# Packed GLA level scores and softmax attention's values moved ahead of the transposes, in a two-layer decoder trunk

## What is computed

```
# GLA, per head and chunk: decayed scores, causal
A   = einsum('bihk,bjhk,bijhk->bhij', q, k, exp(b_i - b_j)) for j <= i
o   = (q * exp(b)) @ S + A @ v

# softmax attention, per block of 128 queries and a window of 256 keys
s = q @ k.T * HEAD_DIM ** -0.5 + bias ;  m = max(max(s), sink)
p = exp(s - m) ;  p = p / (sum(p) + exp(sink - m))
o = p @ v
```

## Time and profile before

| | us |
|---|---|
| median of 3 runs (2592.79 to 2594.49) | 2592.86 |
| the profiled execution, its own time | 2590.38 |
| span of its instructions | 2588.6 |
| its mean granted TensorE clock | 0.988 |
| PE, DVE, ACT busy | 2461.5, 1617.4, 1150.7 |
| GLA turns, about 56 to 565 us of the span | 509 |
| softmax attention, about 1384 to 1790 us of the span | 406 |

### The profile page before, as it was taken

One profiled execution on the slowest core, in us unless ns is written; L12 is line 12 of the kernel. 1 busy time (PEld: TensorE's weight loads), 2 busy tenths in 40 slices (PEclk: granted clock), 3 DMA queues, 4 the chain that ended last, 5 costly groups with the idle time before them and its releaser, 6 DMA issues. The chain is left out here.

```text
span 2588.6 us, 37710 instructions
## 1 busy us (share of the span) xinstructions
PE 2461.5 (95%) x15399; PEld 2149.4 (83%) x15399; DVE 1617.4 (62%) x2930; ACT 1150.7 (44%) x1822; POOL 44.1 (2%) x66
## 2 busy tenths in 40 slices
PE   7999999999999999999998999889999999999997
PEld 4777988877888889999996677767788889999996
DVE  5677567675765556766656665655766556655556
ACT  4655454544343334343336666654444333423333
POOL 0000000000000000000000000000000000000000
PEclk9999999999999999999999999989999999999998
DMA  4222222323433323322323232312332323332322
GB/s 158 66 66 89 83 93 98 126 93 97 157 103 120 107 86 97 127 84 89 115 83 95 97 114 71 95 50 79 115 126 95 103 94 98 98 118 79 98 82 97
DMA packets 83592, 255.18 MB, mean 99 GB/s; under 512 B 12963, under 2 KB 30540, under 8 KB 81484
## 3 DMA queue, kind: packets, MB, share of 16 engines
q1 hardware_dynamic: 64348, 202.45, 24.8%
q0 software_dynamic: 5792, 28.05, 3.4%
q10 hardware_dynamic: 13280, 22.28, 2.6%
HBM read 225.93 MB, written 26.74 MB: 98 GB/s over the span
## 5 line engine op out<-in xcount | busy, mean ns | idle before, releaser
L447 PE MATMUL banks<-act_hi,w_lo 128*128 128x272 f32 (+1 forms) x2952 | 972.7, 330 | 16.3 <-DVE act_lo L2295 6.7
L447 PE MATMUL banks<-act_hi,w_hi 128*128 128x272 f32 (+1 forms) x2952 | 958.6, 325 | 0.0
L447 PE MATMUL banks<-act_lo,w_hi 128*128 128x272 f32 (+1 forms) x2952 | 957.0, 324 | 0.0
L425 ACT ACTIVATE w_hi<-w_raw 128x1024 fp32r<-128x1024 f32 x366 | 380.8, 1055 | 691.6 <-PE banks L470 489.4
L430 DVE TENSOR_TENSOR w_lo<-w_raw,w_hi 128x1024 fp32r<-128x1024 f32 x366 | 443.1, 1223 | 367.0 <-ACT w_hi L425 366.7
L447 PEld LDWEIGHTS banks<-act_hi,w_lo 128*128 128x128 f32 x2952 | 557.5, 189 | 75.9 <-issue 20.9
L447 PEld LDWEIGHTS banks<-act_lo,w_hi 128*128 128x128 f32 x2952 | 558.6, 189 | 43.0 <-issue 1.7
L447 PEld LDWEIGHTS banks<-act_hi,w_hi 128*128 128x128 f32 x2952 | 557.1, 189 | 43.9
L482 DVE TENSOR_TENSOR acc<-acc,banks 128x272 f32<-128x272 f32 (+1 forms) x624 | 315.3, 519 | 191.2 <-PE banks L470 187.7
L470 PE MATMUL banks<-h_hi,w_lo 128*128 128x272 f32 (+1 forms) x1056 | 346.7, 328 | 23.0 <-DVE acc L482 13.5
L470 PE MATMUL banks<-h_hi,w_hi 128*128 128x272 f32 (+1 forms) x1056 | 344.6, 326 | 0.0
(11 more groups left out here) (243 smaller groups left out, 2601.6 us busy)
## 6 DMA issues: line engine op xcount, KB each, us to landing
w_raw<-wall SPq DMA_DIRECT2D x366, 512.0 KB, 3.6
normed<-h_scratch POOLq DMA_DIRECT2D x20, 352.0 KB, 4.2
h_scratch<-acc POOLq DMA_DIRECT2D x3, 2176.0 KB, 7.8
h_scratch<-acc POOLq DMA_DIRECT2D x3, 2048.0 KB, 7.7
gstates<-state ACTq DMA_DIRECT2D x4, 1024.0 KB, 6.5
gla_s<-gstates ACTq DMA_DIRECT2D x4, 1024.0 KB, 6.8
bias<-bias_scratch ACTq DMA_DIRECT2D x28, 128.0 KB, 2.4
bias_scratch<-bias_rows ACTq DMA_DIRECT2D x8, 383.0 KB
```

The lines of the kernel that those rows point to most:

```text
L425: nc.scalar.activation(WH[:, b % RING], WR[:, b % RAW], ACT.Copy).then_inc(w_hi, 1)
L447: last = nc.tensor.matmul(PS[:, bank, 0:n], w, a[X][:, k, o:o + n], start=(k == 0 and first), stop=(k == KT - 1 and w is wh and a is AH))
```

## The change

Four edits. In GLA, levels 1 to 4 stream only the right halves of the query blocks, 64 columns for each chunk in place of 128, into the first 256 columns of the bank, DVE's `masked` reads them there, and the zeroing of `QT[1]` goes. In `values` and in `s_values` the loop over e becomes the inner one, so that output partitions 0 to 63 and 64 to 127 take turns. PE's `s_new(d)` and `values(s - 3)` move from behind the projections of an iteration to between `scores(s)` and `transposed(s - 2)`. DVE's `s_new(d)` moves within w = 5 from behind `biased(s)` and the additions to ahead of `biased(s)`.

```diff
@@ -718,7 +718,12 @@
                         pe.wait_ge(dn_add, dn_end(("gla", u - 1)))
                     for c in range(HB):
                         x = slice(c * CH, (c + 1) * CH)
-                        last = nc.tensor.matmul(PS[:, 6 + s % 2, x], KTl[s % 2][:, x], QT[s % 2][:, x], start=True, stop=True)
+                        out, queries = PS[:, 6 + s % 2, x], QT[s % 2][:, x]
+                        if s:
+                            L = LEVELS[LV[s]]
+                            out = PS[:, 6 + s % 2, c * (CH // 2):(c + 1) * (CH // 2)].rearrange("p (n s) -> p n s", s=L)
+                            queries = queries.rearrange("p (n s) -> p n s", s=2 * L)[:, :, L:2 * L]
+                        last = nc.tensor.matmul(out, KTl[s % 2][:, x], queries, start=True, stop=True)
                     if s == 0 and X:
                         pe.wait_ge(v_ev_, VR[u, 1, 1])
                         x = slice(HP, HP + SAMP)
@@ -959,7 +964,7 @@
                 L = LEVELS[n]
                 nb = CH // (2 * L)
                 mask = MLEV[:, n].rearrange("p (n s) -> p n s", s=2 * L)[:, :, L:2 * L].unsqueeze(1).broadcast_to([P, HB, nb, L])
-                scores = PS[:, 6 + s % 2].rearrange("p (c n s) -> p c n s", c=HB, s=2 * L)[:, :, :, L:2 * L]
+                scores = PS[:, 6 + s % 2, 0:HP // 2].rearrange("p (c n s) -> p c n s", c=HB, s=L)
                 nc.vector.tensor_tensor(TM[:, s % 2].rearrange("p (c n s) -> p c n s", c=HB, s=L), scores, mask,
                                         ALU.mult).then_inc(lv_m, 1)
 
@@ -1002,7 +1007,6 @@
                         nc.vector.scalar_tensor_tensor(SB[:, b], SB[:, b], EL[:, 8 + b:9 + b], PS[:, 6 + b % 2, 0:DV],
                                                        ALU.mult, ALU.add).then_inc(ss_upd, 1)
 
-                nc.vector.memset(levels_of(QT[1], LEVELS[0])[0], 0.0)
                 nc.vector.memset(levels_of(KTl[1], LEVELS[0])[1], 0.0)
                 decayed(u, 1)
                 distance(u, 2)
@@ -1701,8 +1705,8 @@
                     if X and g % 8 == 2:
                         pe.wait_ge(xsa, 3 * (g // 8 - 4) + 1)
                 o, n = WIN * (g % 2), HD * (q % 8 // 4)
-                for e in range(2):
-                    for k in range(x0 // WIN, 2):
+                for k in range(x0 // WIN, 2):
+                    for e in range(2):
                         last = nc.tensor.matmul(PS[64 * e:64 * e + 64, 4, o:o + WIN], VTOK[:, blk - 1 + k, n:n + HD],
                                                 PT[:, g % 2, 2 * e + k], start=(k == x0 // WIN), stop=(k == 1))
                 last.then_inc(of, 1)
@@ -1789,10 +1793,12 @@
             def s_values(d):
                 pe.wait_ge(xte, 3 * d + 3)
                 pe.wait_ge(vc_in, 16 * (d // 2) + 16)
+                for b in range(NB):
+                    for e in range(2):
+                        y = slice(64 * e, 64 * e + 64)
+                        nc.tensor.matmul(PS[y, 7, 0:2 * SAMP], VCG[:, b], PX[:, b, y], start=(b == 0), stop=False)
                 for e in range(2):
                     y = slice(64 * e, 64 * e + 64)
-                    for b in range(NB):
-                        nc.tensor.matmul(PS[y, 7, 0:2 * SAMP], VCG[:, b], PX[:, b, y], start=(b == 0), stop=False)
                     last = nc.tensor.matmul(PS[y, 7, 0:2 * SAMP], VTOK[0:SAMP, 8, HD * (d // 2):HD * (d // 2) + HD], PXN[:, y],
                                             start=False, stop=True)
                 last.then_inc(xof, 1)
@@ -1807,6 +1813,10 @@
                     scores(s)
                 if s == 0:
                     pe.wait_ge(dn_add, dn_end((1, FG - 1)))
+                if d >= 0 and w == 4 and d < 4:
+                    s_new(d)
+                if 3 <= s < NIT + 3:
+                    values(s - 3)
                 if 2 <= s < NIT + 2:
                     transposed(s - 2)
                 if k == 0:
@@ -1823,10 +1833,6 @@
                 if w >= 4 and 1 <= k < 8:
                     units = len(down_units((k - 1) // 4)) // 4
                     downs(k - 1, range((w - 4) * units, (w - 3) * units))
-                if d >= 0 and w == 4 and d < 4:
-                    s_new(d)
-                if 3 <= s < NIT + 3:
-                    values(s - 3)
                 if s in (21, 22):
                     by_token(s - 21)
                 if d >= 0:
@@ -1944,6 +1950,8 @@
                     divided(s - 1)
                 if s >= 4 and s % 2 == 1:
                     lo(s - 4)
+                if d >= 0 and w == 5:
+                    s_new(d)
                 if s < NIT:
                     biased(s)
                 for q in range(1, PAIRS):
```

## The result

| | before | after |
|---|---|---|
| median, us (4 runs each, side by side) | 2592.82 (2590.65 to 2594.49) | 2637.07 (2635.33 to 2638.51) |
| span of the profiled execution | 2588.6 | 2635.2 |
| mean granted TensorE clock | 0.988 | 0.978 |

The ratio is 1.0175, with an interval from 1.0159 to 1.0190: slower by 44 us. The forecast was 2608, slower by 15, with a range that ended at 2622. The sign and the mechanism came out as forecast; the size is three times the forecast's and lies outside the range.

The account below looks back on a forecast made before the run. In-order PE, busy 2461.5 of 2588.6 us, was taken as the bound. New waits and clock, +23.6, less savings of 8.5, gave net +15.1 on 2592.9, so 2608 us; range 2588 to 2622.

Parts of the forecast that it names:

- Order in `values` 0, in `s_values` -5.2: Inner loop over e: nothing gained in `values`; each of four `s_values` calls 1.3 us shorter, -5.2 us in all.
- Shape changes -1.2: PE in attention: one change of stationary shape fewer where sample transposes follow the projection, -1.2 us.
- w = 7 with samples: Iterations 47, 55, 63 and 39: `values` wait 4.3 us for `lo` (6.5 at 39); together +9.8 us net.
- 21, 29, 31: Iterations at w = 5 and 7 with nothing late: `values` wait 0.5 us each for `lo`, +1.5 us.
- the clock: PE's granted clock at half after waits of 2 us or more: two added stretches of 3.4 us, +2 (0 to +7).
- the half X = 0: Iterations 5 to 25, norms and residual on DVE: eleven waits of 18.6 us in place of 13.0, +5.6 us.
- the iterations after w = 7 (41, 49, 57): DVE reaches its tail 2 us later because it waits for PE's down units: 0 to +5.4, middle taken, +2.7 us.
- s_new: -2.1: PE's four waits for DVE's `s_new`, 3.1 us, shrink to some 0.25 each when it moves ahead of `biased`: -2.1 us.
- 51, 59, 61: Iterations late by norm steps, most of it paid already by `te` or a bank: +2.0 us.
- A: Rival: waiting at `values` lets DVE catch up, so later waits vanish equally; only the 8.5 us gain remains, 2584; chance 0.15.
- C: Rival, half the waits: the half X = 0, 51, 59, 61 and the iterations after w = 7 cost nothing; 2596; chance 0.10.
- D: Rival, worse: all bounds at their upper end and no overlap in `s_values`, +28 us, 2621; chance 0.11.

Follow-up runs that it names:

- experiment 2: Kernel before, with only the loop order of e and k or b in `values` and `s_values` changed: 2585.47 us, ratio 0.9979.
- Experiment 7: Changed kernel plus 116 useless matmuls of 256 columns in 18 odd iterations, just ahead of the wait for `lo`: 2622.1 us, ratio 1.0114.
- Experiment 9: Changed kernel with DVE's norm steps of iterations 12 and 14 run ahead of its additions of the down units: 2633.88 us, ratio 1.0164.
- Experiment 5: Changed kernel with PE's `values` back at their old place, `s_new` still moved on both engines: 2585.55 us, ratio 0.9974.
- experiment 6: Changed kernel with `values` moved in even iterations only, at their old place in odd ones: 2583.87 us, ratio 0.9967.

## Why the forecast was right in kind and wrong in size

**Right.** *GLA at 0*: 0.9996. *Order in `values` 0, in `s_values` -5.2*: -5.4 alone; the call measured 1.34 us in the changed kernel, in three of the four, and 2.31 in the one that met a stretch at half clock. The Trainium skill's rule on row groups (TensorE: Matmul & The Clock Gate, The mechanism) would have kept 2.60; the measured 1.30 decides against it here. The forecast's step from `values` was weaker than it looks, though. Its 0.112 us is the pace of loads of 128 columns; `values` and `s_values` load 64, and in the earlier trace rows these go at (1619.54 - 1618.52) / 16 = 0.064. Eight at 0.064 take 0.5 us before the last one's way through, so the 0.67 of `values` shows no overlap by itself. That the price came out is in part luck; the overlap is shown by experiment 2. *Shape changes -1.2*: only in the aggregate, -6.6 us of work where -6.4 was forecast. *The mechanism*: odd iterations wait for `lo`, the change's own row of 62.7 us. *w = 7 with samples*: forecast 4.3, three times, and 6.5 at 39. Iteration 47 in the changed kernel, PE, then DVE and ACT:

```profile
1670.09 0.70 PE L1684 MATMUL banks<-kg,q 64*128 64x256 f32 x4
1675.21 0.96 PE L1710 MATMUL banks<-probs_t,v_tok 128*64 128x128 f32 x8 [4.42 <-DVE o_lo L1895]
```

```profile
1670.20 0.44 DVE L480 COPY acc<-banks 128x272 f32<-128x272 f32 x1 [0.32 <-PE banks L470]
...
1671.27 1.28 DVE L1923 CUSTOM_DVE_ANT_1 s_scores<-s_scores,s_mask,s_sinks 128x1024 f32<-128x1024 f32 x1
...
1672.89 1.17 ACT L2073 ACTIVATE s_scores<-s_scores,s_stats 128x1056 f32<-128x1056 f32 x1 [4.37 <-DVE s_stats L1927]
...
1674.25 0.36 ACT L2051 ACTIVATE o_hi<-banks 128x256 fp32r<-128x256 f32 x1
...
1674.64 0.42 DVE L1895 TENSOR_TENSOR o_lo<-banks,o_hi 128x256 fp32r<-128x256 f32 x1 [1.71 <-ACT o_hi L2051]
```

It is the chain of the earlier trace rows, instruction by instruction. The four waits measure 6.47, 4.42, 4.42 and 4.43. *21, 29, 31*: 1.9 us in all, forecast 1.5. *The banks' waits that go*: forecast -6, measured -8.9.

**Wrong 1, the clock: "I add two such stretches, at somewhat over half price: +2 (0 to +7)".** Measured +16. The step's premise was that most new waits stand where one was. But the waits grew in number (22 for `lo` where there were 3), and the stretches in number and length: nine of 37.5 us became sixteen of 88.7, ten of them 6.8 us long. The price was about right: 2 us for two stretches of 3.4 is 0.29 for each microsecond at half, where 0.32 to 0.36 came out. The count was wrong: 51 us more at half are fifteen stretches of 3.4, where the forecast had two. It was read from a single row of before, which has nine in the stage, two of them 6.8 us long. This is 14 of the 35 us that the forecast fell short in the stage.

**Wrong 2, the half X = 0: 18.6 us of new waits.** Measured 26.9 (4.12 at 5, 1.88 at 7, 0.87 at 8, 1.93 at 11, 3.42 at 13, 6.01 at 15, 1.99 at 17, 1.62 at 19, 3.09 at 23, 1.99 at 25), and none at 9, where 2.2 were forecast. With the 13.0 of before that is +13.9 in place of +5.6. The step that failed is "what counts is the chain from biased(s - 2) to the end of lo(s - 4) against PE's work": it took the chain's length from the kernel before. DVE in the kernel before, from biased(13) to lo at the head of 15:

```profile
1445.81 0.48 DVE L1875 CUSTOM_DVE_ANT_0 scores<-banks,bias,sinks_b 128x256 f32<-128x256 f32 x1
...
1450.29 0.69 DVE L480 COPY acc<-banks 128x512 f32<-128x512 f32 x1 [1.41 <-PE banks L470]
1451.68 0.69 DVE L480 COPY acc<-banks 128x512 f32<-128x512 f32 x1 [0.70 <-PE banks L470]
...
1457.74 0.41 DVE L1889 TENSOR_TENSOR o_lo<-banks,o_hi 128x256 fp32r<-128x256 f32 x1
```

The same in the changed kernel:

```profile
1451.30 0.47 DVE L1881 CUSTOM_DVE_ANT_0 scores<-banks,bias,sinks_b 128x256 f32<-128x256 f32 x1
...
1456.23 0.69 DVE L480 COPY acc<-banks 128x512 f32<-128x512 f32 x1 [4.04 <-PE banks L470]
1458.03 0.69 DVE L480 COPY acc<-banks 128x512 f32<-128x512 f32 x1 [1.11 <-PE banks L470]
...
1461.01 0.69 DVE L480 COPY acc<-banks 128x512 f32<-128x512 f32 x1 [1.43 <-PE banks L470]
1462.41 0.69 DVE L480 COPY acc<-banks 128x512 f32<-128x512 f32 x1 [0.70 <-PE banks L470]
1463.02 2.48 DVE L586 TENSOR_TENSOR act_lo<-normed,act_hi 128x1088 fp32r<-128x1088 f32 x2
1465.60 2.87 DVE L571 SCALAR_TENSOR_TENSOR normed<-acc,gain_cols,rstd 128x544 f32<-128x544 f32 x4
...
1468.47 0.40 DVE L1895 TENSOR_TENSOR o_lo<-banks,o_hi 128x256 fp32r<-128x256 f32 x1
```

The chain is 1468.87 - 1451.30 = 17.6 us, where it had been 1458.15 - 1445.81 = 12.3, and 7.3 of it are idle times in which DVE waits for PE, where there were 2.1: DVE's own work is 10.2 and 10.3. The largest of them, 4.04, stands where PE's down units go at half clock, 0.43 us apart in place of 0.23:

```profile
1454.28 0.63 PE L470 MATMUL banks<-o_hi,w_hi 128*128 128x512 f32 x1
1454.71 0.63 PE L470 MATMUL banks<-o_hi,w_lo 128*128 128x512 f32 x1
...
1459.89 0.40 PE L470 MATMUL banks<-o_hi,w_hi 128*128 128x512 f32 x1
1460.12 0.39 PE L470 MATMUL banks<-o_hi,w_lo 128*128 128x512 f32 x1
```

After each wait of PE, DVE has caught up; its additions then hang on PE's down units, and what follows the last of them (5.35 us of norm steps, then `lo`) lies whole behind PE's last unit, and so whole in PE's next wait. The chain is no length of DVE's own: it stretches with PE. The forecast saw this at w = 7 of the samples, and got the size there; it did not look for it here. Experiment 7 parts the two. There the clock is full at this place and the chain only 15.0 us long (1453.43 to 1468.42), but the values of 15 start as late after their scores, 1468.47 - 1461.85 = 6.6 us, as in the changed kernel, 1469.01 - 1462.30 = 6.7:

```profile
1461.85 0.70 PE L1685 MATMUL banks<-kg,q 64*128 64x256 f32 x4
1462.48 5.45 PE L1705 MATMUL banks<-kg,ident 128*128 128x256 f32 x24
1468.47 0.44 PE L1713 MATMUL banks<-probs_t,v_tok 128*64 128x128 f32 x4 [0.55 <-DVE o_lo L1898]
```

So the tail behind PE's last unit sets the wait, not the chain's length. Experiment 9 shows a part of it only: 3.0 us of these two waits go with another order, the rest is DVE's work.

**Wrong 3, the iterations after w = 7 (41, 49, 57).** "I take the middle, +2.7": 6.0 measured, a little over the bound of 5.4. It is the same feedback, and with it the upper end was the reasoned one.

**Wrong 4, s_new: -2.1.** Experiment 5 against 2 gives -1.3 us by the ratios, and their intervals hold both 0 and -2.1. With `values` moved as well, the waits show no gain but a loss of 1.7 us. The three microseconds that went came back in `s_scores`, whose bank `s_add` reads. Timeline of the changed kernel, DVE, then PE:

```profile
1603.47 0.68 DVE L1916 TENSOR_TENSOR s_scores<-banks,s_bias 128x512 f32<-128x512 f32 x1
```

```profile
1604.21 1.07 PE L1766 MATMUL banks<-kcg,q_sample 64*64 64x512 f32 x4 [1.38 <-DVE s_scores L1916]
```

Ahead of these scores stood `values` and the wait for `s_new`, which gave `s_add` its time. The forecast asked what covers the work that moves in, not what the work that moves out had been covering: +4.8 us in the change.

**Wrong 5, 51, 59, 61: +2.0.** Their waits of values are 2.34, 6.21 and 4.59. In the trace of before nothing stood at 51, 4.46 for `turned` at 59, and 1.95 for an addition at 61; and the wait of 3.74 for an addition at 52 became 2.96. That is +6.0, so here little was paid already. With the other groups, 10.1 + 6.0 + 13.9 + 1.9 + 4.8 - 3.1 = 33.6, it makes 39.6 of the 39.9.

**The rivals.** A (the stalls only change place) falls, though some did: 8.9 us of banks' waits and 12.1 of those for `turned` (12.3 + 2.6 in the list of before, 1.9 + 0.9 now) went; but 57 us of waits for `lo` came. (The forecast's "the 12.3 us neither go nor grow" was wrong, for most of them went into the later wait for `lo`; its groups took them off all the same.) C falls with it. D, worse by all upper ends, was the nearest and its 28 us still fell short: its clock term ended at 7 of 16, and the largest group, the half X = 0, had no upper end at all. Since every group depends on the same feedback, the ends go together, and the range should have reached past their sum.

## What to carry to other kernels

Before work is moved ahead in an in-order engine, list what it waits for in each phase of the loop, and move it only where that is already met: half of this move, in even iterations, cost nothing, and the other half some 50 us. Where the producer's program has a tail that itself hangs on the waiting engine's last piece of work, everything behind that piece on the producer is the wait, whatever the trace of before shows as its length. And price the clock with the waits: here 40 us of waits brought 16 us of lower clock.

## What was not expected of the hardware

Useless matmuls in the waits make the kernel 15 us faster (experiment 7), and the clock granted in the stage goes from 0.90 to 0.98. In the stage each stretch at half clock, 9 before and 16 after, begins during a wait of PE of 1.9 us or more or within 2 us behind one, and is 3.4 or 6.8 us long. The reverse does not hold: two waits of 1.99 us in the changed kernel and one of 2.65 in experiment 6 have no such stretch behind them, and one of 1.5 in experiment 2 has one, so no least length of a wait can be read from these traces. A microsecond at half costs 0.32 us by the fit of the stage's sum and 0.36 by the starts, not 0.5. In the changed kernel only 70.0 of the 88.7 us at half are starts that follow each other without a wait, and these lose 31.7, or 0.45 for each of the 70.0; the others are mostly waits, in which the clock costs nothing.
